# Attention bias by matrix products, and the last two expert blocks summed on the chip

## The reference

```python
h = _rms(x, norm1_g) * (1.0 + sc1) + sh1
z = h @ w_in
rec = _hgrn2(rq, rf, ri, rg, lb, rec_out_g)            # 4 heads of 128
# attention, 8 heads of 64, for blocks of 128 queries
score = sum_h relu(iq_h @ ik.T) * iw_h                 # indexer; the best 64 keys are kept
logits = q @ k.T * 64 ** -0.5 + rel_bias[_t5_bucket(idx - t)]
p = softmax(where(valid, logits, -inf)); att = _rms(p @ v, attn_out_g)
x = x + g1 * (concat([rec, att]) @ w_out)
h2 = _rms(x, norm2_g) * (1.0 + sc2) + sh2
# 4 groups x 4 experts; two experts of one group for each row
y = sum_e combine[:, e] * ((silu(h2 @ w1[e]) * (h2 @ w3[e])) @ w2[e])
x = x + g2 * y
```

## Time and profile before

| | |
|---|---|
| median of 3 runs | 1978.87 us (1978.68 to 1980.58) |
| the profiled execution | 1979.37 us, span 1977.7 us |
| PE busy | 1833.2 us (93%) |
| DVE busy | 1387.4 us (70%) |
| ACT busy | 951.4 us (48%) |
| POOL busy | 156.5 us (8%) |
| mean granted clock of TensorE | 0.961 |

### The profile page before, as it was taken

How to read it: one execution, slowest core, us unless ns; L and a number is a source line. 1 busy time by engine, 2 the same in 40 slices (tenths; PEclk the granted TensorE clock), 3 DMA queues, 4 the chain that set the end, 5 groups by cost and what they waited for, 6 DMA issues and landing times.

```text
span 1977.7 us, 31346 instructions
## 1 busy us (share of the span) xinstructions
PE 1833.2 (93%) x12367; PEld 1690.2 (85%) x12367; DVE 1387.4 (70%) x1438; ACT 951.4 (48%) x871; POOL 156.5 (8%) x147
## 2 busy tenths in 40 slices
PE   7999899998999799989999899988995589999995
PEld 7999799997999699979999799966994478888884
DVE  6444786857766644467785776676687698888884
ACT  4343556433443443436563334433344357777773
POOL 1000000000000000000000000000000034324301
PEclk9999999998999899989999899988997789999997
DMA  6555454654766445544556376734340289999993
GB/s 238 191 191 184 141 207 170 230 177 147 293 247 240 155 172 189 191 152 170 190 186 239 140 265 251 252 141 151 126 133 20 73 312 359 357 363 365 353 365 130
DMA packets 61900, 418.21 MB, mean 211 GB/s; under 512 B 7312, under 2 KB 7680, under 8 KB 13936
## 3 DMA queue, kind: packets, MB, share of 16 engines
q1 hardware_dynamic: 51392, 369.19, 51.0%
q0 software_dynamic: 10400, 47.73, 6.9%
q10 hardware_dynamic: 16, 0.01, 0.0%
HBM read 405.88 MB, written 11.02 MB: 211 GB/s over the span
## 4 chain that ended last, share of the span: by engine, by line
PE 84%; DVE 7%; DVEq 3%; issue 2%; ACT 1%; DMA 1%; POOL 1%; ACTq 0%; POOLq 0%
PE ps L1619 15%; PE ps L1621 15%; PE ps L1620 15%; PE ps L1681 4%; PE ps L1682 4%; PE ps L1685 4%; PE ps L801 4%; PE ps L802 4%; PE ps L803 4%; PE ps L830 2%; PE ps L785 2%; PE ps L832 2%; PE ps L831 2%; DVEq L2038 1%; PE ps L1723 1%
## 5 line engine op out<-in xcount | busy, mean ns | idle before, releaser
L1993 DVE TENSOR_TENSOR wlo<-raw,whi 128x2048 fp32r<-128x2048 f32 x236 | 538.4, 2291 | 337.1 <-ACT whi L1836 334.2
L1619 PE MATMUL ps<-xThi,whi 128*128 128x256 f32 x2272 | 644.5, 284 | 1.4 <-DVE xTlo L2004 1.4
L1620 PE MATMUL ps<-xTlo,whi 128*128 128x256 f32 x2272 | 643.8, 283 | 0.0
L1621 PE MATMUL ps<-xThi,wlo 128*128 128x256 f32 x2272 | 643.8, 283 | 0.0
L1836 ACT ACTIVATE whi<-raw 128x2048 fp32r<-128x2048 f32 x236 | 449.9, 1910 | 399.8 <-PE ps L1621 259.0
L1619 PEld LDWEIGHTS ps<-xThi,whi 128*128 128x128 f32 x2272 | 436.9, 192 | 4.0 <-DVE xTlo L2004 1.8
L1620 PEld LDWEIGHTS ps<-xTlo,whi 128*128 128x128 f32 x2272 | 436.9, 192 | 1.8 <-issue 0.2
L1621 PEld LDWEIGHTS ps<-xThi,wlo 128*128 128x128 f32 x2272 | 436.9, 192 | 0.0
L1359 DVE TENSOR_TENSOR wlo<-raw,whi 128x2048 fp32r<-128x2048 f32 x76 | 175.1, 2305 | 19.3 <-ACT whi L992 18.9
L992 ACT ACTIVATE whi<-raw 128x2048 fp32r<-128x2048 f32 x76 | 145.6, 1917 | 48.1 <-PE ps L803 25.7
L801 PE MATMUL ps<-whi,xsel_hi 128*128 128x512 f32 x304 | 120.4, 396 | 0.8 <-ACT xsel_hi L1021 0.8
(11 more groups left out here) (459 smaller groups left out, 2979.4 us busy)
## 6 DMA issues: line engine op xcount, KB each, us to landing
raw<-stream SPq DMA_DIRECT2D x236, 1024.0 KB, 4.9
raw<-experts SPq DMA_DIRECT2D x76, 1024.0 KB, 7.5
mod<-experts SPq DMA_DIRECT2D x38, 1024.0 KB, 7.2
adaraw<-ada POOLq DMA_DIRECT2D x24, 1024.0 KB, 5.1
yd<-lnrow POOLq DMA_DIRECT2D x19, 512.0 KB, 8.6
lnrow<-ln_g POOLq DMA_DIRECT2D x6, 512.0 KB, 5.2
lnrow<-ln_b POOLq DMA_DIRECT2D x6, 512.0 KB, 6.6
x_sb<-x SPq DMA_DIRECT2D x1, 1024.0 KB, 5.2
```

The source lines that it names most:

```text
L1619: nc.tensor.matmul(outs[tile], wh, xh[:, k, :], start=k == 0, stop=False)
L1620: nc.tensor.matmul(outs[tile], wh, xl[:, k, :], start=False, stop=False)
L1621: last = nc.tensor.matmul(outs[tile], wl, xh[:, k, :], start=False, stop=k == KD - 1)
L1993: v.tensor_tensor(wlo[:, slot, :], raw[:, slot, :], whi[:, slot, :].bitcast(F32), ALU.subtract).then_inc(lo_done, 1)
```

## The change

**The bias.** The table `hank` is loaded by one DMA in natural order of the distances (`rel = arange - 255`) and the heads. A new constant `flip` is the identity with its rows reversed. `bias(i)` on TensorE clears the banks of the logits by products with `zero_w` and then adds `flip.T @ hank` for each head; the logits' own products add to that. So `choose(i)` ends with the mask in `score`, and `mask(i)` adds the mask (broadcast over the heads) to PSUM. `bias(0)` is ahead of the transposes of q and k, `bias(1)` behind the logits of i = 0.

**`cat`.** The recurrent half's product with its gate goes from VectorE to GpSimd. ScalarE copies `qkT` ahead of that half's scaling. The attention half's last norm is done for each i apart (`att_norm`), that of i = 0 without the squares of i = 1. The low split of the last weight unit goes behind `cat_lo(2)` and `cat_lo(3)`.

**The last two blocks** (`FAR` = 17, and 18). Their outputs are no more stored. `far_shares` makes for each of them a 128x128 matrix of shares (row's share where its slot is in the block, else 0), transposed by `turn_shares`, and `far_products` multiplies it with `ybuf` in f32 into banks 5, 6, 7 and 0. Slots past the first 17 blocks are read from a row of zeros, `yd[FAR_SLOT]`, which GpSimd writes early. So the gathers and the sums of the near rows (`near_sum`) begin when block 16 is stored. GpSimd holds the gathers until the low part of unit (18, 3) is made, ScalarE its scalings until that of (17, 4), since they use the raw buffers. ScalarE's near scaling stands behind its last high part, `hThi` of block 18. The output pieces go left halves first.

```diff
+            def bias(i):
+                pe.wait_ge(ev[f"relu{i}"], 1)
+                for b in range(2 + 2 * i):
+                    mm(bank(4 - 4 * i + b), zero_w[:, :], xThi[:, 0:2, :].rearrange("p k t -> p (k t)"), start=True, stop=False)
+                for h in range(A_HEADS):
+                    mm(spans(i)[:, pos(h), :], flip[:, :], hank[:, h, T - SPAN[i]:T], start=False, stop=False)
+
+            pe.wait_ge(ev["hank_in"], 16)
+            bias(0)
             pe.wait_ge(ev["qk_norm"], 1)
...
-                              qkT[head_rows(h), 4 + h // 2, 0:SPAN[i]], start=True, stop=True)
+                              qkT[head_rows(h), 4 + h // 2, 0:SPAN[i]], start=False, stop=h in LAST_IN_BANK[i])
                 last.then_inc(ev[f"lg{i}_ps"], 1)
                 if i == 0:
+                    bias(1)
                     pe.wait_ge(x_done, 4 * N_CAT + 2)
...
+            pool.wait_ge(ev["rec_scaled"], 1)
+            nc.gpsimd.tensor_tensor(cat[:, :, 0:512], cat[:, :, 0:512], gate[:, :, :], ALU.mult).then_inc(x_done, 2)
...
-                dve.wait_ge(ev["hank_in"], 32)
-                backwards = hank[:, :, 0:n][:, :, ::-1]
-                v.tensor_tensor(logits(i), backwards, score[:, i:i + 1, 0:n].to_broadcast([P, A_HEADS, n]), ALU.add)
-                dve.drain()
...
-                v.tensor_tensor(logits(i), spans(i), logits(i), ALU.add)
+                n = SPAN[i]
+                v.tensor_tensor(logits(i), spans(i), score[:, i:i + 1, 0:n].to_broadcast([P, A_HEADS, n]), ALU.add)
...
             choose(0)
-            dve.wait_ge(ev["rec_scaled"], 1)
-            v.tensor_tensor(cat[:, :, 0:512], cat[:, :, 0:512], gate[:, :, :], ALU.mult).then_inc(x_done, 2)
             mask(0)
...
-            turn(BASE, OFF_WOUT2)
+
+            att_norm(0)
+            att_norm(1)
             cat_lo(2)
             cat_lo(3)
+            turn(BASE, OFF_WOUT2)
...
+            def far_products(b):
+                n = b - FAR
+                for half in range(2):
+                    pe.wait_ge(ev["y_right"], FAR + 2 + (1 + half if n else 0))
+                    for i in range(TT):
+                        ins = mm(bank(FAR_BANKS[2 * half + i]), share[:, n, i, :], ybuf[:, b % 2, 512 * half:512 * half + 512],
+                                 start=n == 0, stop=n == 1)
+                        if n == 1:
+                            ins.then_inc(ev["far_ps"], 1)
...
+                if b < FAR:
+                    store(b)
+            unit_split(pool, expert_unit(BLOCKS - 1, 3))
+            for b in (FAR - 2, FAR - 1):
                 pool.wait_ge(stored[b % 2], stored_to(b))
...
+                if b == BLOCKS:
+                    act.wait_ge(ev["weighed"], 1)
+                    unit_split(act, expert_unit(FAR, 4))
+                    for i in range(TT):
+                        act.wait_ge(back[i], 32)
+                        act_fn(raw[:, 2, i * D:(i + 1) * D], raw[:, i, 0:D], ACT.Identity,
+                               scale=rt[:, i, 33:34]).then_inc(ev["first_w"], 1)
...
+                if b == FAR:
+                    far_shares()
...
+                if b == BLOCKS:
+                    dve.wait_ge(ev["y_left"], FAR + 1)
+                    v.tensor_tensor(ybuf[:, FAR % 2, 0:512], ybuf[:, FAR % 2, 0:512], row(mod, 5)[:, 0:512],
+                                    ALU.mult).then_inc(ev["y_right"], 1)
+                    near_sum(0, 0)
+                    near_sum(0, 1)
+                    near_sum(1, 1)
...
+            near_sum(1, 0)
+            dve.drain()
+            for half in range(2):
+                cs = slice(512 * half, 512 * half + 512)
+                for i in range(TT):
+                    n = 2 * half + i
+                    dve.wait_ge(ev["far_ps"], n + 1)
+                    v.tensor_tensor(x[:, i, cs], x[:, i, cs], bank(FAR_BANKS[n]), ALU.add).then_inc(ev["final"], 1)
```

More of the change, by code:

```diff
@@ L536, in pool_block2 @@
             sc = t["scratch"]
-            for b in range(2):
-                pool.dma_start(hank[:, 4 * b:4 * b + 4, :], bass.AP(
-                    tensor=sc.tensor, offset=sc.offset + b * HANK + 1, ap=[[1, P], [2 * HANK, A_HEADS // 2], [1, T]])
-                               ).then_inc(ev["hank_in"], 16)
+            pool.dma_start(hank[:, :, :], bass.AP(tensor=sc.tensor, offset=sc.offset, ap=[[1, P], [HANK, A_HEADS], [1, T]])
+                           ).then_inc(ev["hank_in"], 16)
+            pool.wait_ge(ev["rec_scaled"], 1)
+            nc.gpsimd.tensor_tensor(cat[:, :, 0:512], cat[:, :, 0:512], gate[:, :, :], ALU.mult).then_inc(x_done, 2)
             pool.wait_ge(x_done, 4 * N_CAT + 4)
@@ L672, in pe_block2 @@
                 last.then_inc(ev[f"sc{i}_ps"], 1)
+            LAST_IN_BANK = [[max(h for h in range(A_HEADS) if pos(h) * SPAN[i] // 512 == b) for b in range(2 + 2 * i)]
+                            for i in range(TT)]
+            def bias(i):
[6 more added lines that the diff above has]
+            bias(0)
             pe.wait_ge(ev["qk_norm"], 1)
@@ L833, in outputs, with turn_shares @@
                 last.then_inc(used, 1)
+            def turn_shares():
+                pe.wait_ge(ev["shares_in"], 1)
+                for n in range(2):
+                    for i in range(TT):
+                        last = nc.tensor.transpose(bank(5, (2 * n + i) * P, (2 * n + i + 1) * P),
+                                                   tests[:, i, n * SLOTS:(n + 1) * SLOTS], eye[:, :])
+                last.then_inc(ev["shareT_ps"], 1)
+            def far_products(b):
+                n = b - FAR
+                for half in range(2):
+                    pe.wait_ge(ev["y_right"], FAR + 2 + (1 + half if n else 0))
[4 more added lines that the diff above has]
+                            ins.then_inc(ev["far_ps"], 1)
             for group in range(8):
@@ L929, in act_block2 @@
                     root(1, 0, 8, P, "rec_std")
+            act.wait_ge(ev["qkT_ps"], 1)
+            for i in range(TT):
+                ins = act_fn(qkT[:, :, i * P:(i + 1) * P], xT_banks(i), ACT.Copy)
+            ins.then_inc(ev["qkT"], 1)
             act.wait_ge(ev["rec_norm"], 1)
@@ L936, in act_block2 @@
             ins.then_inc(ev["rec_scaled"], 1)
-            act.wait_ge(ev["qkT_ps"], 1)
-            for i in range(TT):
-                ins = act_fn(qkT[:, :, i * P:(i + 1) * P], xT_banks(i), ACT.Copy)
-            ins.then_inc(ev["qkT"], 1)
             def cat_hi(j):
@@ L1458, in dve_block2 @@
             first_one_hot(0)
-            v.tensor_copy(slot_i[:, :, :], slot[:, :, :]).then_inc(ev["slots"], 1)
+            v.tensor_scalar(far[:, :, :], slot[:, :, :], float(FAR_SLOT), None, ALU.subtract)
+            v.tensor_scalar(slot_i[:, :, :], slot[:, :, :], float(FAR_SLOT), None, ALU.min).then_inc(ev["slots"], 1)
             def freed(b, j):
@@ L1494, in dve_block2, with far_shares, near_sum @@
             v.tensor_tensor(R(33, 35), R(33, 35), R(3, 4).to_broadcast([P, TT, 2]), ALU.mult).then_inc(ev["weighed"], 1)
+            def far_shares():
+                dve.wait_ge(ev["oneh"], BATCHES - 2)
+                other = share[:, :, :, :].rearrange("p n i s -> p n (i s)")
+                for i in range(TT):
+                    v.tensor_scalar(tests[:, i, :], iota[:, :], far[:, i, 0:1], rt[:, i, 33:34], ALU.is_equal, ALU.mult)
+                    v.tensor_scalar(other[:, i, :], iota[:, :], far[:, i, 1:2], rt[:, i, 34:35], ALU.is_equal, ALU.mult)
+                dve.drain()
+                for i in range(TT):
+                    ins = v.tensor_tensor(tests[:, i, :], tests[:, i, :], other[:, i, :], ALU.add)
+                ins.then_inc(ev["shares_in"], 1)
+            def near_sum(i, half):
+                dve.wait_ge(ev["first_w"], i + 1)
+                cs = slice(512 * half, 512 * half + 512)
+                acc = raw[:, 2, i * D + 512 * half:i * D + 512 * half + 512]
+                v.scalar_tensor_tensor(acc, raw[:, i, D + 512 * half:D + 512 * half + 512], rt[:, i, 34:35], acc,
+                                       ALU.mult, ALU.add)
+                dve.drain()
+                if half == 0:
+                    v.tensor_tensor(acc, acc, row(mod, 5)[:, cs], ALU.mult)
+                    dve.drain()
+                v.tensor_tensor(x[:, i, cs], x[:, i, cs], acc, ALU.add)
             for b in range(BLOCKS + 1):
```

98 lines of the change are left out of this document (56 added, 42 removed).

## The result

| | before | after |
|---|---|---|
| median | 1979.03 us (1978.68 to 1980.58, 4 runs) | 1960.1 us (1958.98 to 1964.22, 4 runs) |
| profiled execution | 1979.37 us, span 1977.7 | 1959.83 us, span 1958.1 |

The ratio is 0.9907, 95% interval 0.9895 to 0.9918: faster by 18.9 us. The forecast was 1959.0, range 1956 to 1966.

The account below looks back on a forecast made before the run. TensorE bounds most of the run, so gains come only where it waits: the second block's attention and the tail. Terms sum to -20.0 us from 1979.37, giving 1959.4 (1958.9 against the median); forecast 1959.0, range 1956 to 1966.

Parts of the forecast that it names:

- (a): Second block's attention: `choose(0)` loses its bias addition and `cat*gate` goes to GpSimd, so masking begins earlier: -2.5 us.
- (b): Second block's attention: `choose(1)` loses its addition of 2.29 us and the gap: -2.4 us.
- (c): TensorE's added clearing and bias products in attention: 0 on the path; without the cover of its wait, up to 4.5 us.
- (d): GpSimd's multiply of `cat` and gate in attention: takes 3.0 us, ends at 1495, costs +0.3 us (bounds 0 to +9).
- rival 3: GpSimd's multiply in attention is late or holds VectorE in `head_sums(1)`: 1960 to 1966 us; chance 0.15.
- (e): End of attention: normalisation is split, row block 0's scaling goes ahead: -0.7 us on the last `cat`.
- (f): Last weight unit's low split behind `cat_lo(2,3)`: shorter TensorE gap, clock up, router loads sooner; -3.1 us (bounds 0 and -3.1).
- rival 2: Router stage gives nothing: clock falls in the 1.6 us gap or loads land late; +3.1, 1962.1 us; chance 0.17.
- The expert stage: Added instructions and transposes in the expert stage: +0.2, +0.2 and +0.44 us.
- the three small terms: Expert stage: one more 128x4 instruction +0.2, `far_shares` ahead of `hTlo(16)` +0.2, four more transposes +0.44 us.
- The tail: Behind TensorE's last expert product: last two blocks not stored, gathers already landed; end 10.3 us later in place of 22.7: -12.4.

Follow-up runs that it names:

- Experiment 5: Changed kernel with the product of `cat` and its gate moved from GpSimd back to VectorE, between `choose(0)` and `mask(0)`: 1963.13 us, ratio 0.9922.
- experiment 4: Changed kernel without the six clearing products; the first bias product of each bank starts the sum: 1960.45 us, ratio 0.9903.
- e_no_clear: Same run as experiment 4: changed kernel without the six clearing products: 1960.45 us, ratio 0.9903.
- e_gather_late: Changed kernel with GpSimd's gathers held until the low part of unit (18, 5), not (18, 3): 1967.17 us, ratio 0.9930.
- Experiment 6: Changed kernel with the low split of the last weight unit back ahead of `cat_lo(2)` and `cat_lo(3)`: 1963.78 us, ratio 0.9925.
- e_front_only: Kernel before with the attention half of the change alone; the tail is that of before: 1971.03 us, ratio 0.9957.
- e_tail_only: Kernel before with the expert half of the change alone (shares, far products, early near sums, last two blocks not stored): 1969.73 us, ratio 0.9944.
- e_gap_fill: Changed kernel with two far products of block 17's right half put into TensorE's last wait, ahead of `outputs(18, 4)`: 1958.23 us, ratio 0.9900.
- e_warm_router: Changed kernel with zero products filling TensorE's router waits (34, 18 and 14 of them): 1958.98 us, ratio 0.9894.
- experiment 11: Same run as `e_warm_router`: changed kernel with zero products filling TensorE's router waits: 1958.98 us, ratio 0.9894.
- e_best: Changed kernel with new tiles behind the one-hot tiles, attention and router waits filled, and one far product in TensorE's last wait: 1956.13 us, ratio 0.9882.
- experiment 8: Same run as `e_gather_late`: changed kernel with GpSimd's gathers held until the low part of unit (18, 5): 1967.17 us, ratio 0.9930.

## Why the prediction was right

By its own steps, measured from the start of `choose(0)`:

- **(a)** -2.5 forecast, -2.5 measured. Experiment 5 gives VectorE's product its 1.2 to 1.5 us; the addition of 1.23 is the rest.
- **(b), (c)** -2.4 and 0; together -2.7. The clearing products cost nothing on the path (experiment 4). But the cover that I named was thinner than I worked out: 8.29 less 4.9 leaves 3.4 us (3.1 with the 5.2 measured), and 1.05 was left. The clock fell to 0.50 in 1505 to 1515, and 4.2 us went with it (the weighing of i = 0 took 3.65 us in place of 1.97, `wout(0)` 8.2 in place of 5.7); 2.1 came back, as that weighing began 2.1 us earlier against the start of `choose(0)`. I had not priced a clock that falls elsewhere. Where the clock falls under `turn_probs(1)` as well, it is on the path: in `e_no_clear` and `e_gather_late` the exponentials' start to the second evacuation took 32.9 us in place of 28.5. The changed kernel's run of 1964.22 is probably such a one; it has no trace.
- **(d)** 3.0 us and +0.3 forecast; 2.35 us, and no cost that the traces show. The idle time that rival 3 feared did not come: the product began 0.16 us behind the end of the scaling. The estimate of 2.2 worked out from the Trainium skill (GPSIMD Engine Reference, Performance versus the Vector engine) was nearer than my value between rows.
- **(e), (f)** -0.7 and -3.1, so -3.8 between the exponentials and the second evacuation; measured -4.3 (28.49 for 32.81). The last `cat` came 1.1 us of it sooner, the rest lies behind it. The gap is 1.41 us (1.6 forecast), the clock stays at 1.00, the load lands in 2.8 us (3.5 forecast). Of the rest 1.3 us are the shorter gap, 1.6 the clock and 0.4 the load. Experiment 6 gives back the first two, 2.8 us; the landing, one of the two ways in which rival 2 let this term fail, moved 4 us there at no cost.
- **Not forecast:** -1.2 us between the second evacuation and the one-hot tiles. I had no term there, and its instructions are the same. It belongs to the attention half (28.95 us in `e_front_only`, 30.32 in `e_tail_only`), and the traces show where it lies. The 24 products of the router's scores, before and after:

```profile
1569.18 0.41 PE L751 MATMUL ps<-xTlo,rwhi 128*20 128x256 f32 x1
```

```profile
1561.22 0.28 PE L781 MATMUL ps<-xTlo,rwhi 128*20 128x256 f32 x1
```

Before, the first half of them took 0.41 us each, at half clock; after, all took 0.28, and the last began 2.7 us behind the first in place of 3.9. Why the clock rose sooner there is open.
- **The expert stage** +0.84 forecast, +2.2 measured: the one term that was mis-sized by more than half. With the addresses of before it is 370.24 against 369.57 in the kernel before, so +0.7, as the three small terms say. The other 1.5 come from where the two new tiles were put. That step of the prediction left the allocation out.
- **The tail** -12.4 forecast, -12.7 measured. Eight f32 products took 7.03 us against the 7.0 worked out from the earlier trace rows, and near sums, evacuation and gathers ended in the order forecast; the end is 10.05 us behind the end of TensorE's last expert product (10.40 behind its start) against 10.3.

The sum was 1.2 us short of the -21.2 measured and the later start of `choose(0)` took 1.6 back, so 1959.83 beside 1959.4. Part of the nearness is therefore luck: errors of -2.3 ahead of the experts and +1.4 in them, and an offset that no part of the change made. It is luck, too, that three of the four executions took the shorter length: the trace of `e_no_clear`, on the longer course of the clock, ends 6.3 us later from the start of `choose(0)`, and no term of the sum holds that.

## What to carry to other kernels

Ask of every cover not only how long it is but at which clock the engine under it runs: 10 us at half clock ate 4 us of slack with the same instructions. Put new tiles behind the ones that the long loops read, and compare the mean time of an untouched product before and after; 5 ns on 456 products was more than all the new work of that stage. Order a split that frees large loads behind the small loads that someone waits for, but ask first what that wait is worth: the chain that ended last names one path, and here another ended 0.4 us ahead of it. Compare traces in distances from a common instruction, not in times of the span: the start of this stage moved by 2.8 us between programs that are the same up to it.

## What the runs showed of the hardware

**Two courses of the clock.** The same kernel runs at one of two lengths some 5 us apart: the changed one at 1958.98 to 1960.37 and once 1964.22; `e_gap_fill` at 1956.80, 1957.08, 1958.23 and at 1962.85, 1962.98; `e_gather_late` at 1962.27, 1962.87 and 1967.17 to 1967.94. In the traces the longer ones (`e_no_clear`, `e_gather_late`, `e_warm_router`) have the second evacuation 62.0 to 62.1 us behind the start of `choose(0)`, the shorter 57.7; the first two are 1.9 us longer in the router as well. Windows of `e_no_clear`:

```profile
1506.00:1514.00 8.00, 7.31 (x20) 5.80 (x21) 7.19 (x16) 0.64 (x2) 0.00 (x0) 0.59 0.00 0
...
1519.00:1524.00 5.00, 4.89 (x24) 4.42 (x24) 2.70 (x10) 3.19 (x8) 0.00 (x0) 0.54 0.00 0
1524.00:1530.00 6.00, 6.00 (x24) 5.47 (x24) 3.23 (x11) 1.49 (x3) 0.00 (x0) 0.53 0.01 3
```

TensorE is busy for 10.89 of 11 us in the last two and has 0.53. The clock fell there at 1519.4, behind a wait of 1.47 us and a stretch (1514 to 1518) with 2.43 of 4 us busy, and was back at 1529.6. TensorE was busy without a break from 1520 to 1529, and the clock stayed at 0.50 all that time. What picks the course stays open: `e_gap_fill` and `e_gather_late`, identical up to this point, began `choose(0)` at 1486.84 and 1486.70 and waited 1.09 and 1.14 us for the exponentials, and only in the second did the clock fall.

**Filled waits move a dip.** With the router's waits filled, the clock stayed up in the router and fell at the start of the experts, 2.6 us dearer (experiment 11); in `e_best` it did not come there.

**GpSimd's gathers and VectorE.** An indirect gather was issued in 0.94 to 1.03 us by itself and in 2.45 to 2.83 beside VectorE's splits, ending 0.8 us behind the split each time (experiment 8). The tail bears it, with under 2 us to spare.

**A tile's place.** Shifting the three tiles behind by 2064 bytes in each row made 128x512 products that read two of them 1.3% longer (395 against 390 ns). Why this place and not the other, the runs do not say.
